# Turning the stage input by token tile, and ordering the last output products by token tile, in a twelve-stage transformer kernel

## The reference

```
x = layer_norm(ALPHA*x + mix)          # stages s5, sb (mixers)
x = layer_norm(ALPHA*x + ffn + ple)    # stages moe0, moe1
x = x + mixer(rms_norm(x))             # stages conv0, lru, mla, conv1
x = x + swiglu_ffn(rms_norm(x))        # stages ffn0 .. ffn3
```

## Time and profile before

| | |
|---|---|
| median of three runs | 2444.24 us |
| profiled execution, own time | 2444.77 us |
| its span | 2442.1 us |
| TensorE matmul busy | 2223.9 us (91%) |
| VectorE busy | 1589.6 us (65%) |
| ScalarE busy | 1199.7 us (49%) |
| DMA, mean over the span | 185 GB/s |

### The profile page before, as it was taken

The page is one execution under the profiler, slowest core; times in us unless marked ns, Lnnn a source line. Parts: engine busy times, 40 slices in busy tenths (PEclk is TensorE's granted clock), DMA queues, the critical chain, the costliest instruction groups (busy, mean ns, idle before and its releaser), DMA issues.

```text
span 2442.1 us, 29583 instructions
## 1 busy us (share of the span) xinstructions
PE 2223.9 (91%) x11242; PEld 1871.2 (77%) x11242; DVE 1589.6 (65%) x2084; ACT 1199.7 (49%) x1489; POOL 40.0 (2%) x41
## 2 busy tenths in 40 slices
PE   5479999997999999999899997699985899999999
PEld 5258887776977888777798887688874788888887
DVE  7976558888537556888765558755557554566554
ACT  3125446775453545777445444554443354444443
POOL 1220000000000000000000000000000000000000
PEclk9688999998998999999899999899997899999999
DMA  6023568997503557999456554355631156545663
GB/s 248 18 78 132 190 197 310 339 359 266 189 19 110 174 182 241 354 347 347 156 174 198 186 179 140 100 182 182 196 129 52 50 180 193 182 163 172 198 192 101
DMA packets 123164, 452.17 MB, mean 185 GB/s; under 512 B 13808, under 2 KB 13808, under 8 KB 122128
## 3 DMA queue, kind: packets, MB, share of 16 engines
q1 hardware_dynamic: 121680, 442.55, 53.7%
q0 software_dynamic: 1056, 6.95, 0.8%
q10 hardware_dynamic: 288, 0.80, 0.1%
HBM read 449.19 MB, written 1.05 MB: 184 GB/s over the span
## 4 chain that ended last, share of the span: by engine, by line
PE 78%; DVE 13%; ACT 3%; issue 2%; DMA 2%; POOL 1%; SPq 0%; ACTq 0%; DVEq 0%; POOLq 0%
PE bank L298 20%; PE bank L300 19%; PE bank L299 19%; DVE w_lo L274 4%; PE bank L291 4%; PE bank L292 4%; PE bank L293 4%; DMA raw<-in_stream 2%; ACT w_hi L267 1%; DVE scr L2256 1%; PE bank L583 1%; DVE scr L2240 1%; PE bank L1017 1%; DVE scr L1625 1%; PE bank L2066 0%
## 5 line engine op out<-in xcount | busy, mean ns | idle before, releaser
L274 DVE TENSOR_TENSOR w_lo<-raw,w_hi 128x1024 fp32r<-128x1024 f32 x840 | 1003.3, 1223 | 531.0 <-ACT w_hi L267 527.8
L267 ACT ACTIVATE w_hi<-raw 128x1024 fp32r<-128x1024 f32 x840 | 875.3, 1058 | 722.6 <-PE bank L300 541.5
L298 PE MATMUL bank<-w_hi,x_hi 128*128 128x512 f32 x1024 | 403.6, 394 | 4.8 <-DVE x_lo L493 4.8
L299 PE MATMUL bank<-w_lo,x_hi 128*128 128x512 f32 x1024 | 400.5, 391 | 0.0
L300 PE MATMUL bank<-w_hi,x_lo 128*128 128x512 f32 x1024 | 400.4, 391 | 0.0
L298 PE MATMUL bank<-w_hi,c_hi 128*128 128x512 f32 x872 | 344.0, 394 | 43.2 <-issue 21.1
L299 PE MATMUL bank<-w_lo,c_hi 128*128 128x512 f32 x872 | 341.9, 392 | 0.0
L300 PE MATMUL bank<-w_hi,c_lo 128*128 128x512 f32 x872 | 341.8, 392 | 0.0
L291 PE MATMUL bank<-x_hi,w_hi 128*128 128x256 f32 x792 | 227.8, 288 | 25.6 <-DVE w_lo L274 20.9
L298 PEld LDWEIGHTS bank<-w_hi,x_hi 128*128 128x128 f32 x1024 | 193.6, 189 | 44.8 <-issue 5.6
L298 PEld LDWEIGHTS bank<-w_hi,c_hi 128*128 128x128 f32 x872 | 165.2, 189 | 80.8 <-issue 46.5
(11 more groups left out here) (397 smaller groups left out, 2251.1 us busy)
## 6 DMA issues: line engine op xcount, KB each, us to landing
raw<-in_stream SPq DMA_DIRECT2D x840, 512.0 KB, 4.3
ln_rows<-in_ln POOLq DMA_DIRECT2D x4, 1024.0 KB, 5.0
scr<-in_xt SPq DMA_DIRECT2D x1, 1024.0 KB, 5.1
scr<-in_s POOLq DMA_DIRECT2D x1, 1024.0 KB, 12.2
x<-in_x POOLq DMA_DIRECT2D x1, 1024.0 KB, 17.1
out_x<-x SPq DMA_DIRECT2D x4, 256.0 KB, 2.8
par<-in_par ACTq DMA_DIRECT2D x1, 752.5 KB, 9.2
scr<-in_ple POOLq DMA_DIRECT2D x1, 512.0 KB, 9.3
```

The source lines that it names most:

```text
L267: nc.scalar.activation(w_hi[:, n % RING, :], raw[:, n % RING, :], ACT.Copy).then_inc(hi_done, 1)
L274: nc.vector.tensor_tensor(w_lo[:, n % RING, :], raw[:, n % RING, :], w_hi[:, n % RING, :].bitcast(F32), ALU.subtract).then_inc(lo_done, 1)
L298: nc.tensor.matmul(out, xh, hi, start=start, stop=False)
L299: nc.tensor.matmul(out, xh, lo, start=False, stop=False)
```

## The change

- **Last output products.** `outer_pe` joins the last two visits to weight tiles, and `last_down` the last two weight tiles of an ffn stage: all their slabs for token tile 0, then all for token tile 1.
- **Turning.** `turn_x(pe, st, tt, q)` turns one half (four chunks) of one token tile into bank 2*tt + q. Where both stages are of the RMS kind, the two halves of token tile 0 are turned behind the third-last and the second-last slab of token tile 1.
- **Ffn next.** If the next stage is an ffn, token tile 1 is turned only inside that stage's first weight tile, between the slabs of token tile 0 and those of token tile 1. Otherwise it is turned behind the last slab.
- **Rounding.** `x_hi` and `x_lo` are made half by half of a token tile: with a gain four instructions of 128 x 128 instead of two of 128 x 256, without a gain one of 128 x 512 as before. There is one signal for each half. ScalarE squares a token tile behind its roundings.
- **VectorE's order** in an RMS close is add, add, `x_lo(0,0)`, add, `x_lo(0,1)`, add, `x_lo(1,0)`, `x_lo(1,1)`.
- **moe.** The routing product, and the ranks, write bank 0 instead of bank 3; the gate product's halves swap banks.

```
@@ close_pe: the turns
+        def turn_x(pe, st, tt, q):
+            b = Q[2 * tt + q]
+            before(pe, b)
+            pe.wait_ge(dve_did["x"], dve_did.at("x", st, tt, q))
+            for c in range(4):
+                last = nc.tensor.transpose(b[:, c * P:(c + 1) * P], x[:, tt, (4 * q + c) * P:(4 * q + c + 1) * P], column("ident", 0, P))
+            last.then_inc(pe_did["x turned"], pe_did.next("x turned", st, tt, q))
+            after(b, ("dve", ("x_lo", st, tt, q)))
...
-            for b in Q:
-                before(pe, b)
             for tt in range(TT):
-                for i in range(4):
...
+                for q in range(2):
+                    early = tt == 0 and kind(st) == "rms" and kind(st + 1) == "rms"
+                    late = tt == 1 and by_token_next(st)
+                    if not early and not late:
+                        turn_x(pe, st, tt, q)
@@ close_act
+            for tt in range(TT):
+                for q in range(2):
+                    act.wait_ge(pe_did["x turned"], pe_did.at("x turned", st, tt, q))
                     if nxt == "raw":
-                        last = nc.scalar.activation(pair(x_hi, i), bank(Q[i]), ACT.Copy)
+                        last = nc.scalar.activation(chunks_of(x_hi, tt, q), four(Q[2 * tt + q]), ACT.Copy)
                     else:
                         name, at = gain(st + 1)
-                        for c in (2 * i, 2 * i + 1):
-                            last = nc.scalar.activation(x_hi[:, c, :], bank(Q[i])[:, c % 2, :], ACT.Copy, scale=column(name, at + c))
+                        for c in range(4):
+                            last = nc.scalar.activation(x_hi[:, 4 * q + c, tokens(tt)], four(Q[2 * tt + q])[:, c, :], ACT.Copy,
+                                                        scale=column(name, at + 4 * q + c))
...
+                if nxt == "rms":
+                    square_x(act, st, tt)
@@ close_dve (rest_of_x makes x_lo of one half of a token tile, add_y one addition)
+            if stages[st][0] not in LN_STAGES:
+                add_y(dve, st, 0, 0)
+                add_y(dve, st, 0, 1)
+                if nxt == "rms":
+                    rest_of_x(dve, st, 0, 0)
+                add_y(dve, st, 1, 0)
+                if nxt == "rms":
+                    rest_of_x(dve, st, 0, 1)
+                add_y(dve, st, 1, 1)
+                if nxt == "rms":
+                    rest_of_x(dve, st, 1, 0)
+                    rest_of_x(dve, st, 1, 1)
                 return
@@ input_ready
+                if st:
+                    if k % 4 == 0:
+                        for tt in tiles:
+                            pe.wait_ge(dve_did["x_lo"], dve_did.at("x_lo", st - 1, tt, k // 4))
@@ ffn_pe
                         if first == 0:
+                            if u == 0 and tt == 1 and label == "h1":
+                                turn_x(pe, st - 1, 1, 0)
+                                turn_x(pe, st - 1, 1, 1)
                             before(pe, banks[tt])
...
+            def last_down(u):
+                part = widths[u] // (2 * P) - 1
+                tiles = take_tile(), take_tile()
+                pe.wait_ge(dve_did["h_lo"], dve_did.at("h_lo", st, u, part))
+                for tt in range(TT):
+                    for c, n in zip((2 * part, 2 * part + 1), tiles):
+                        for half in range(2):
+                            down_slab(u, c, n, tt, half)
+                            if tt == 1 and kind(st + 1) == "rms" and (c, half) in ((2 * part, 1), (2 * part + 1, 0)):
+                                turn_x(pe, st, 0, half ^ 1)
@@ moe_pe
-            logits = Q[3][:, 0:2 * TT * N_EXPERTS].rearrange("p (t j e) -> p t j e", t=TT, j=2)
-            before(pe, Q[3])
+            logits = Q[0][:, 0:2 * TT * N_EXPERTS].rearrange("p (t j e) -> p t j e", t=TT, j=2)
+            before(pe, Q[0])
@@ outer_pe
+            visits = [list(group) for _, group in groupby(slabs, key=lambda s: s[0])]
+            if k_last in ks:
+                visits[-2:] = [visits[-2] + visits[-1]]
...
+                        if tt == 1 and k_last in ks and group is visits[-1] and kind(st) == "rms" and kind(st + 1) == "rms" and i >= len(group) - 3 and i < len(group) - 1:
+                            turn_x(pe, st, 0, i - len(group) + 3)
```

More of the change, by code:

```diff
@@ L50 @@
 LN_STAGES = ("s5", "moe", "sb")
+BY_TOKEN = ("ffn",)
 def stage_blocks(stage):
@@ L440, in square_x, with add_y, rest_of_x @@
                 act_did["x squared"], act_did.next("x squared", st, tt))
+        def add_y(dve, st, tt, half):
+            dve.wait_ge(pe_did["y"], pe_did.at("y", st, tt, half))
+            part = x[:, tt, half_of(half)]
+            nc.vector.tensor_tensor(part, part, Y[2 * tt + half][:, :], ALU.add).then_inc(
+                dve_did["x"], dve_did.next("x", st, tt, half))
+        def rest_of_x(dve, st, tt, q):
+            b = Q[2 * tt + q]
+            dve.wait_ge(act_did["x_hi"], act_did.at("x_hi", st, tt, q))
+            if kind(st + 1) == "raw":
+                last = nc.vector.tensor_tensor(chunks_of(x_lo, tt, q), four(b), chunks_of(x_hi, tt, q).bitcast(F32), ALU.subtract)
+            else:
+                name, at = gain(st + 1)
+                for c in range(4):
+                    k = 4 * q + c
+                    last = nc.vector.scalar_tensor_tensor(x_lo[:, k, tokens(tt)], four(b)[:, c, :], column(name, at + k),
+                                                          x_hi[:, k, tokens(tt)].bitcast(F32), ALU.mult, ALU.subtract)
+            last.then_inc(dve_did["x_lo"], dve_did.next("x_lo", st, tt, q))
         def close_dve(dve, st):
@@ L475, in close_dve @@
                                                        ALU.mult, ALU.add).then_inc(dve_did["x"], dve_did.next("x", st, tt, half))
[L476 to L482, removed]
-            nxt = kind(st + 1)
-            if nxt == "end":
-                return
[L486 to L495, removed]
+            nxt = kind(st + 1)
+            if stages[st][0] not in LN_STAGES:
[10 more added lines that the diff above has]
+                    rest_of_x(dve, st, 1, 1)
+                return
+            for tt in range(TT):
+                for q in range(2):
+                    rest_of_x(dve, st, tt, q)
         def first_x_act(act):
@@ L770, in moe_pe @@
                     for tt in range(TT):
-                        b = Q[2 * half + tt]
+                        b = Q[2 * (1 - half) + tt]
                         before(pe, b)
@@ L1217, in outer_pe @@
                                             k == k_first, k == k_last)
-                        end = tt == TT - 1 and b == group[-1][1] and (b == BLOCKS_PER_TILE - SLAB or k == k_last)
+                        end = tt == TT - 1 and last_of_tile and (b == BLOCKS_PER_TILE - SLAB or k == k_last)
                         if k == k_last:
```

85 lines of the change are left out of this document (45 added, 40 removed).

## The result

The changed kernel takes 2458.16 us (median of 4, 2457.40 to 2459.75) beside 2443.30 (4, 2438.99 to 2445.59): ratio 1.0064 [1.0046, 1.0081]. It is slower, within the range, and 4 us above the predicted time. The medians lie 14.9 us apart; the sum had said 9.8. The profiled execution took 2458.77 us (span 2457.0), 14.0 more than that of before, and its span is 14.9 us longer. TensorE's share of the chain is 78% as in the earlier trace rows.

A forecast was written before the change was run, and what follows sets the result against it. The prediction took TensorE's standstill at the stage closes as the bound, with VectorE's chain at layer-norm closes. It summed 12.1 - 4.5 + 2.2 = +9.8 us to 2454.0 us, range 2444 to 2460.

The forecast's parts named there:

- RMS closes without the clock, +12.1: Seven closes between RMS stages: new waits, turns and narrow roundings add 12.1 us in all, clock falls not counted.
- conv0 to ffn0: RMS close into an ffn stage: TensorE waits of 0.7, 0.5 and 1.6 us plus sixteen transposes, +1.55 us.
- Half-width pitch 0.26 and 0.25: 128-wide roundings with a gain at RMS closes: one every 0.26 us on VectorE, every 0.25 on ScalarE.
- rival 2: Narrow roundings are cheap: at a pitch of 0.20 the seven closes cost 5.6 us, total 2445.5; chance 0.13.
- Layer-norm closes, -4.5: Four layer-norm closes: earlier VectorE chains and routing products outweigh later x_lo(1,0), together saving 4.5 us.
- sb to moe1: Layer-norm close into moe1: chain starts 1.1 us earlier, routing product gains 2.3 more, sum -3.4 us.
- s5 to moe0: Layer-norm close into moe0: the chain gains a wait of 0.43 us, the routing product 2.3; sum -2.7 us.
- moe0 to sb: Layer-norm close out of moe0: x_lo(1,0) stands third in VectorE's line, costing +0.4 us.
- moe1 to conv0: Layer-norm close out of moe1: four-fold roundings, with x_lo(1,0) third in line, cost +1.2 us.
- The clock, +2.2: Closes ffn to lru, mla, conv1: two clock falls in three closes at 1.1 us each; bounds 0 to 7.
- rival 4: More clock falls, also in the ffn closes: 2460 us or more; chance 0.05.
- Rival 1: Moe stages: the routing product starts before the clock falls and holds it, saving 11 us, total 2440.6; chance 0.12.

The follow-up runs named there:

- rms_fill: The changed kernel with unread 256-wide matmuls filling TensorE's waits at the closes of RMS stages; 2451.41 us, 1.0034 of the kernel before.
- no_late: The changed kernel without late turns: token tile 1 is turned at the close, not inside the next ffn stage; 2452.64 us, 1.0036 of the kernel before.
- after: The changed kernel itself, as profiled, against the kernel before; median 2458.16 us, ratio 1.0064.
- ln_fill: The changed kernel, all closes but the two into moe set back, plus unread 256-wide matmuls in the layer-norm closes' waits; 2430.27 us, 0.9953 of before.
- after_again: The changed kernel measured again, nothing altered, as reference for its group; 2457.97 us, 1.0061 of the kernel before.

## Why the prediction was right, and where it was wrong

- **RMS closes without the clock, +12.1**: right in place and size. rms_fill measures 13.1. At conv0 to ffn0 the waits in brackets sum to 2.5 us and the forecast was 2.8, yet the close cost 1.7 and not 1.55. A bracket begins at the end of the row before it, some 0.16 us behind the point from which the next matmul could start (rows of 0.39 start 0.227 apart); counted from the starts the three are 3.0.
- **Half-width pitch 0.26 and 0.25**: measured 0.26 and 0.27; rival 2 (0.20) falls.
- **Layer-norm closes, -4.5**: measured -5.0. sb to moe1 -3.2 for -3.4. s5 to moe0 -3.7 for -2.7: the product began 2.3 us sooner (184.06 for 186.36) and the wait of 0.43 is gone, as forecast; the other 1.0 is a clock that came back sooner (at 193.8 for 198.1), and in no_late, the same program up to there, it comes back at 195.9 and the close gives -2.2. moe0 to sb +1.0 for +0.4: 0.4 is the wait, and more of sb's first product stands at half clock, 3.0 us for 1.8. moe1 to conv0 +0.9 for +1.2. All four in no_late: -3.5.
- **The clock, +2.2, is the step that failed.** I let it fall at two of three closes for 1.1 us each. It fell at all three, and at two of the four closes into an ffn stage, which rival 4 had at 0.05; and a fall of 3.4 us cost 1.6, one of 6.8 us cost 2.0 to 2.5. Measured 9.8 (some 7 by the medians). The total still came near because the clock in sb gave back 2.9 us and that in moe0 1.0, neither of them forecast; that part is luck, not reasoning. Rival 4, more falls, is what happened at the closes.
- **Rival 1** (the clock stays up in the moe stages) did not come about: TensorE still idles 2.14 us ahead of the turns of token tile 1, and the clock is down when the product starts. What the forecast of this rival left out is that the fall itself can come sooner: before it came at 764.7 (the rival says 764.9), in after at 756.9. ln_fill removes that idle time; the product of moe1 then runs at full clock to its end, and the clock falls 0.9 us behind it. The Trainium skill (TensorE: Matmul & The Clock Gate, "Part 1: The HAM clock gate") says the gate is set by how busy TensorE has been recently. The fillers agree. The routing product does not: from 756 to 760 us TensorE is busy 3.96 of 4.00 us, and the clock falls at 760.8. Busy is the profile's measure here (rows of 0.26 us that start 0.11 apart); whether the gate takes it so, no run shows.

Open: why the clock fell at conv0 to ffn0 and mla to ffn2 and not at lru to ffn1 and conv1 to ffn3, whose gaps are the same (0.66, 0.16 and 1.70 us beside 0.66, 0.17 and 1.68). It is no chance of one execution, since after_again falls at the same five closes, and in no_late it is the other two of these four that fall; no run tells the cause.

## What to carry to other kernels

Work that is split so that half of it can start sooner has a price in its second half: here the closes were bound by VectorE's queue, and splitting lengthened the roundings in it by a third (4.22 us for 3.23). Ask of each gap not only how long TensorE stands, but how little of TensorE's other work is left in it: one wait of 1.3 us, cut into three with turns between, lost the clock at five of seven closes, and that cost 9.8 us beside 13.1 for the rest. Where a wait can't be removed, unread wide matmuls into a free bank are a cover, worth some 7 us by the medians here; and look for the dull part of a change (here the bank of one small product), which was worth 3.2 us alone.

## What the runs showed of the hardware

- TensorE, busy without a gap, lost its clock during a product of matmuls of 32 and 16 columns (ln_fill, 187.4 us in moe0), and 0.9 us behind such a product (760.8). With one 256-wide matmul to two narrow ones it fell too (186.1, 762.9), with three it stayed (1.00 from 182 to 194 and 755 to 767 us).
- Matmuls whose operands never change held the clock: 8, 6 and 5 of them in gaps of 1.2, 0.9 and 0.9 us were enough (rms_fill), as were 60 in a gap of 7.6 us (ln_fill).
- A matmul of 32 or 16 columns is issued every 0.11 us at full clock and every 0.21 at half, nearly as a 256-wide one is (0.12 and 0.21): 32 of them took 3.6 us in ln_fill against 6.8.
